# Block 2's attention heads reordered on ScalarE, weight splits behind the exponentials, and tensors moved by 64 and 160 bytes

## The chip, the core and the metric

The kernel runs on one core of a Trainium2 chip. The metric is the device time of one execution in microseconds, lower is better. The engines are TensorE (PE: matrix products, with PEld for its weight loads), VectorE (DVE), ScalarE (ACT), GpSimd (POOL) and the DMA queue that SyncE (SP) feeds.

## What is computed

The reference is a small transformer stack on 256 tokens of width 1024, in float32: two layers of a first block, then two of a second.

```python
def first_block(...):        # 2 layers
    x = x + 0.5 * swiglu(rms_norm(x), w1, w2)          # 1024 -> 2 x 2816 -> 1024
    x = x + hybrid_mixer(rms_norm(x), ...)             # LRU, latent attention, convolution
    x = x + 0.5 * swiglu(rms_norm(x), w1, w2)
def second_block(...):       # 2 layers
    mix = hybrid_mixer_2(rms_norm(x), ...)             # three kinds of attention
    x = x + rms_norm_2(mix)
    x = x + rms_norm_2(conv_ffn(rms_norm(x)))          # 1024 -> 2 x 2816, 3 taps, 2816 -> 1024
def hybrid_mixer_2(h, ...):
    o_fox = fox_attention(...)      # 4 heads, decaying bias from cumulated log_f
    o_nsa = nsa_attention(...)      # 8 heads: compressed keys (gelu MLP), selected blocks, window
    o_dil = dilated_attention(...)  # 4 heads
    return concatenate([o_fox, o_nsa, o_dil]) @ w_out
```

## The kernel before

**Products.** Activations lie as features x tokens: `h_hi` and `h_lo` hold eight tiles of 128 x 256. Every large product is made of three matmuls in a fast float32 format: weights and activations are split into a rounded part and a remainder (`w_hi`, `w_lo`, `h_hi`, `h_lo`), and `product` (L654 to 659) adds hi x hi, hi x lo and lo x hi into one PSUM bank. Each matmul loads a 128 x 128 block of weights and streams 256 columns of the activation. Some products take the weights unsplit in plain float32 (`whole_product`, L704). In `tokens_product` (L706 to 712) the roles change: an activation (`h_hi`, `win_hi`) is the loaded operand, and `w_hi` or `w_lo` is streamed.

**Weights.** All weights come as a stream of units of at most 16 blocks (1 MB). SyncE loads unit s into one of two slots of `raw` (`load_unit`, L580) once the unit two before is split. ScalarE copies it to `w_hi` (`split_hi`, L588 to 606), which waits for the load and for PE to have used the unit four before. VectorE subtracts to `w_lo` (`split_lo`, L629 to 637). PE waits for `w_lo`. The engines' programs say by hand where each split stands in its queue: `split.until(s)` splits all units up to s at that place.

**Where tensors lie.** The tensors are allocated in the order of their declarations, each start on a multiple of 32 bytes. By the program's address map `raw`, `w_hi`, `w_lo`, `x`, `h_hi`, `h_lo`, `const`, `vec`, `scr` and `sq` start at multiples of 128 bytes in each partition. `rinv` has 258 floats, so what follows it starts 32 bytes past such a multiple: `trig1`, `hid_hi`, `hid_lo` (the hidden activations of the FFNs), and, in the same space in other stages, `m_hi`, `m_lo` (block 1's merged branches), `win_hi`, `win_lo`, `o2_hi`, `o2_lo` (block 2). Tiles within them are 1024 bytes apart, blocks of weights 512.

**FFNs.** There are four of block 1 and two of block 2. Each has 22 "up" units of 16 blocks (48 matmuls over `h_hi`, `h_lo`) and 16 "down" units of 11 blocks (33 matmuls over `hid_hi`, `hid_lo`).

**Block 2's mixer.** `second_steps` (L254) writes the order of TensorE's groups by hand: for n from 0 the scores ("S", n), the transposes ("T", n-3), the product with the values ("V" or "W", n-4), and then what `MIX2_BESIDE[n]` puts beside: projections ("f", i), rotations ("R", i), the compression MLP ("ca", "cmp", "ct", "c2"), its attention ("SC", "TC", "J"), the cumulated decays ("cum"), parts of the output projection ("K", i). There are 24 heads. VectorE follows this order (`STEPS2`), ScalarE follows `EVAC2`, which is the same with two steps swapped. For a head ScalarE computes the exponential of n and scales the probabilities of n-1 (step "S", L1741 to 1744), copies the transposed probabilities ("T", L1748) and, at the end of a tile, the output ("W", L1750). "W" n must be copied before the next tile's first "V" may write its bank. VectorE makes the row maximum that the exponential waits for.

```python
EVAC2 = list(STEPS2)
for n in range(3, len(HEADS2)):
    at = EVAC2.index(("S", n))
    EVAC2[at], EVAC2[at + 1] = EVAC2[at + 1], EVAC2[at]
```

So ScalarE's order is T(n-3), S(n), V or W(n-4). In the mixer both splitters run three units ahead of the group in hand (`split.until(at2 + UNIT_OF2[g] + AHEAD)` ahead of the group's own work), and ScalarE also splits ahead of each exponential what `freed_by_scores` (L1678) allows. The units of this stage are, in order, f1, f2, f3, vb0, vb1, f0, f8, va0, va1, f4, f5, ca0, cmp0, ca1, cmp1, f6, f7, O0 to O3; "K" and "O" use O0 to O3. ScalarE's gelu in "cmp" and its exponential need different function tables, which it loads at each change.

## Time and profile before

| | |
|---|---|
| median of 3 runs | 2071.71 us (2068.88 to 2075.6) |
| the profiled execution | 2077.53 us, of which the span is 2075.7 us |
| PE, PEld busy | 1994.5 us (96%), 1898.6 us (91%) |
| DVE, ACT, POOL busy | 1395.0 us (67%), 1159.7 us (56%), 142.6 us (7%) |
| DMA | 329.80 MB, mean 159 GB/s |
| granted TensorE clock | 0.981 of full on average |

The busy time of PE is the sum of matmuls whose ends are modelled and overlap: a matmul of 0.28 us is followed by the next one 0.12 us later. So what a matmul costs is read from start to start, and from how many fall into a stretch, not from its duration. The block 1 layers take the span from 11 to 1280 us, block 2's two layers the rest; the heads of block 2's mixer lie at 1315 to 1468 and at 1710 to 1863 us.

### The profile page before, as it was taken

The page shows a single profiled execution, that of the slowest core. Times are in us where ns is not written, and L with a number is a line of the kernel's source. Part 1 is how long each engine was busy: PE and PEld are TensorE (multiplying, and loading weights), DVE is VectorE, ACT ScalarE, POOL GpSimd, SP SyncE. Part 2 cuts the span into 40 slices and gives each one's busy share as a digit, 9 for nine tenths or more (in the row PEclk, how much of TensorE's full clock was granted, in tenths as well). Part 3 has the DMA queues.
Part 4 walks back from the last instruction along what each step waited for, and adds up shares of the span by engine and source line. Part 5 has one row for each costly group of instructions (what it writes and reads, how often), then busy time and mean ns, then how long its engine had stood idle before and what let it go on. Part 6 is the DMA issues. An engine that isn't in the chain of part 4 may idle for free.

```text
span 2075.7 us, 39521 instructions
## 1 busy us (share of the span) xinstructions
PE 1994.5 (96%) x15240; PEld 1898.6 (91%) x15240; DVE 1395.0 (67%) x2058; ACT 1159.7 (56%) x1847; POOL 142.6 (7%) x153
## 2 busy tenths in 40 slices
PE   7999989999999999999999999998999999899998
PEld 7999988999999999988999999876899998679997
DVE  5765787666655665788666656775698477638963
ACT  5444676564445444676465435665666458556753
POOL 1063100010000001100010001000200010002000
PEclk9999999999999999999999999999999999899999
DMA  5545433455545545443455544531255544203643
GB/s 210 202 166 191 168 127 132 156 189 199 171 168 199 191 154 192 170 150 109 151 193 192 184 156 168 181 123 41 102 187 181 189 144 169 102 24 140 214 156 115
DMA packets 53533, 329.80 MB, mean 159 GB/s; under 512 B 5936, under 2 KB 6704, under 8 KB 27952
## 3 DMA queue, kind: packets, MB, share of 16 engines
q1 hardware_dynamic: 53424, 328.34, 45.4%
q8 instruction: 69, 1.13, 0.2%
q14 instruction: 40, 0.33, 0.0%
HBM read 327.27 MB, written 1.05 MB: 158 GB/s over the span
## 4 chain that ended last, share of the span: by engine, by line
PE 66%; DVE 10%; issue 8%; ACT 5%; DVEq 4%; DMA 4%; POOLq 3%; POOL 1%; ACTq 0%; SPq 0%
PE bank L657 17%; PE bank L658 17%; PE bank L659 17%; PE bank L704 4%; DVE w_lo L636 3%; DMA raw<-in_w 3%; ACT w_hi L597 2%; PE bank L669 1%; PE bank L671 1%; DVE conv L1371 1%; PE bank L1659 1%; PE bank L1643 1%; PE bank L678 1%; DVEq L1365 1%; PE bank L1660 1%
## 5 line engine op out<-in xcount | busy, mean ns | idle before, releaser
L636 DVE TENSOR_TENSOR w_lo<-raw,w_hi 128x2048 fp32r<-128x2048 f32 (+3 forms) x348 | 673.6, 1939 | 326.5 <-ACT w_hi L597 310.6
L657 PE MATMUL bank<-h_hi,w_hi 128*128 128x256 f32 x2704 | 779.8, 288 | 12.2 <-DVE w_lo L636 4.2
L658 PE MATMUL bank<-h_lo,w_hi 128*128 128x256 f32 x2704 | 768.2, 284 | 0.0
L659 PE MATMUL bank<-h_hi,w_lo 128*128 128x256 f32 x2704 | 768.0, 284 | 0.0
L597 ACT ACTIVATE w_hi<-raw 128x2048 fp32r<-128x2048 f32 (+2 forms) x346 | 560.5, 1623 | 138.8 <-DMA raw<-in_w 117.4
L657 PEld LDWEIGHTS bank<-h_hi,w_hi 128*128 128x128 f32 x2704 | 522.2, 193 | 17.6 <-issue 11.7
L658 PEld LDWEIGHTS bank<-h_lo,w_hi 128*128 128x128 f32 x2704 | 522.1, 193 | 1.3
L659 PEld LDWEIGHTS bank<-h_hi,w_lo 128*128 128x128 f32 x2704 | 522.0, 193 | 0.0
L657 PE MATMUL bank<-hid_hi,w_hi 128*128 128x256 f32 x1056 | 295.4, 280 | 0.0
L658 PE MATMUL bank<-hid_lo,w_hi 128*128 128x256 f32 x1056 | 295.4, 280 | 0.0
L659 PE MATMUL bank<-hid_hi,w_lo 128*128 128x256 f32 x1056 | 295.4, 280 | 0.0
L657 PEld LDWEIGHTS bank<-hid_hi,w_hi 128*128 128x128 f32 x1056 | 198.5, 188 | 0.0
L658 PEld LDWEIGHTS bank<-hid_lo,w_hi 128*128 128x128 f32 x1056 | 198.5, 188 | 0.0
L659 PEld LDWEIGHTS bank<-hid_hi,w_lo 128*128 128x128 f32 x1056 | 198.5, 188 | 0.0
L897 ACT ACTIVATE scaled<-scaled 128x256 f32<-128x256 f32 x88 | 36.8, 418 | 257.9 <-DVE scaled L944 257.9
L796 POOL TENSOR_TENSOR acc<-sq 128x256 f32<-128x256 f32 x13 | 12.2, 942 | 1549.4 <-ACT sq L789 1549.1
L1371 DVE SCALAR_TENSOR_TENSOR conv<-glu,vec,conv 128x256 f32<-128x256 f32 x240 | 106.0, 481 | 11.9 <-issue 2.8
L789 ACT ACTIVATE sq<-x 128x256 f32<-128x256 f32 (+1 forms) x88 | 35.9, 410 | 115.2 <-DVE x L974 90.8
L944 DVE TENSOR_TENSOR scaled<-bank,rinv 128x512 f32<-128x512 f32 x88 | 60.6, 689 | 44.8 <-PE bank L659 36.8
L669 PE MATMUL bank<-h_hi,w_hi 128*128 128x256 f32 x224 | 63.4, 316 | 16.0 <-DVEq L1921 6.6
L800 POOL TENSOR_TENSOR acc<-acc,sq 128x256 f32<-128x256 f32 x65 | 60.2, 926 | 222.3 <-ACT sq L789 219.1
L669 PEld LDWEIGHTS bank<-h_hi,w_hi 128*128 128x128 f32 x224 | 49.6, 222 | 18.2 <-issue 10.0
(337 smaller groups left out, 2937.3 us busy)
## 6 DMA issues: line engine op xcount, KB each, us to landing
raw<-in_w SPq DMA_DIRECT2D x198, 1024.0 KB, 4.8
raw<-in_w SPq DMA_DIRECT2D x96, 704.0 KB, 4.1
raw<-in_w SPq DMA_DIRECT2D x52, 768.0 KB, 4.2
raw<-in_w SPq DMA_DIRECT2D x8, 512.0 KB, 3.8
raw<-in_w SPq DMA_DIRECT2D x4, 576.0 KB, 3.7
x<-in_x SPq DMA_DIRECT2D x1, 1024.0 KB, 5.0
out<-x SPq DMA_DIRECT2D x4, 256.0 KB, 2.4
const<-in_const SPq DMA_DIRECT2D x1, 548.0 KB, 5.4
```

The source lines that it names most:

```text
L597: last = act.activation(w_hi[:, s % SPLIT_SLOTS, 0:parted], raw[:, s % RAW_SLOTS, 0:parted], ACT.Copy)
L636: dve.tensor_tensor(w_lo[:, s % SPLIT_SLOTS, 0:n], raw[:, s % RAW_SLOTS, 0:n], w_hi[:, s % SPLIT_SLOTS, 0:n].bitcast(F32), ALU.subtract).t ...
L657: pe.matmul(out, hi, x_hi, start=start, stop=False, skip_group_check=skip)
L658: pe.matmul(out, hi, x_lo, start=False, stop=False, skip_group_check=skip)
L659: return pe.matmul(out, lo, x_hi, start=False, stop=stop, skip_group_check=skip)
L669: pe.matmul(out, w_hi[:, s % SPLIT_SLOTS, at], h_hi[:, k], start=k == 0 and half == 0, stop=False, skip_group_check=half == 1)
L704: return pe.matmul(out, whole_part(s, block, 1), y, start=start, stop=stop)
L789: act.activation(sq[:, parity], src, ACT.Square).then_inc(nm.sq_ready.sem, 1)
L800: pool.tensor_tensor(acc[:], acc[:], sq[:, t % 2], ALU.add).then_inc(nm.sq_summed.sem, 2 if t == KT - 2 else 1)
L897: act.activation(scaled[:, parity, 0:T], scaled[:, parity, 0:T], ACT.Silu).then_inc(silu_ready.sem, 1)
L944: dve.tensor_tensor(halves(scaled[:, parity]), halves(bank[:, :]), by_r(2), ALU.mult).then_inc(work.freed["v"].sem, 1)
L1371: last = dve.scalar_tensor_tensor(conv[:, t], glu[:, t, j:j + T], w, conv[:, t], ALU.mult, ALU.add)
```

## The change

Six things change.

1. `EVAC2`: for n from 4 on, the step S(n) moves two places back instead of one, so ScalarE's order is T(n-3), V or W(n-4), S(n). Head 3 keeps its place.
2. `MIX2_BESIDE`: ("cum", 1) goes from step 13 to 15, ("R", 7) from 14 to 17 (ahead of ("K", 0)).
3. The units cmp0, ca1, cmp1, f6 and f7 no longer make ScalarE and VectorE split three ahead (`SPLIT_BESIDE`). Instead the exponentials of heads 8, 9, 10, 12, 14 are each followed on ScalarE by splits (`HIGH_BEHIND`), and the steps S 9, 10, 11, 12, 16 on VectorE (`LOW_BEHIND`). VectorE's splits up to O3 behind S 14 go.
4. ScalarE splits ahead of the exponential for heads below 8 only.
5. Two unused tensors are added: `offset_h` (64 bytes) ahead of `x`, and `offset_hid` (96 bytes) ahead of the tensors that stages share. `x`, `h_hi`, `h_lo` and all behind move by 64 bytes, `hid_hi`, `hid_lo`, `m_hi`, `win_hi`, `o2_hi` and the like by 160: by the address map all of these then start 64 bytes past a multiple of 128. `raw`, `w_hi` and `w_lo` stay.
6. For the room, `w_lat` holds 21 blocks instead of 22 (`LAT_BLOCKS` 9 instead of 10); one more block of unit ("uq", 2) goes to `sq`.

```diff
-               5: [("win", 4), ("f", 5)], 7: [("ca", 0), ("cmp", 0)], 8: [("ca", 1), ("cmp", 1)], 9: [("ct", 0)],
-               10: [("f", 6), ("c2", 0)], 11: [("cum", 0)], 12: [("SC", 0), ("f", 7)], 13: [("cum", 1), ("R", 6)],
-               14: [("R", 7), ("TC", 0)], 16: [("J", 0)], 17: [("K", 0)], 18: [("K", 1)], 20: [("J", 1)], 21: [("K", 2)], 23: [("K", 3)],
-               25: [("K", 4)], 27: [("K", 5)]}
+               5: [("win", 4), ("f", 5)], 7: [("ca", 0), ("cmp", 0)], 8: [("ca", 1), ("cmp", 1)],
+               9: [("ct", 0)], 10: [("f", 6), ("c2", 0)], 11: [("cum", 0)], 12: [("SC", 0), ("f", 7)], 13: [("R", 6)],
+               14: [("TC", 0)], 15: [("cum", 1)], 16: [("J", 0)], 17: [("R", 7), ("K", 0)], 18: [("K", 1)], 20: [("J", 1)],
+               21: [("K", 2)], 23: [("K", 3)], 25: [("K", 4)], 27: [("K", 5)]}
+HIGH_BEHIND = {8: ("f", 6), 9: ("f", 7), 10: ("O", 0), 12: ("O", 2), 14: ("O", 3)}
+LOW_BEHIND = {9: ("f", 6), 10: ("f", 7), 11: ("O", 0), 12: ("O", 2), 16: ("O", 3)}
+SPLIT_BESIDE = [("cmp", 0), ("ca", 1), ("cmp", 1), ("f", 6), ("f", 7)]
...
-    at = EVAC2.index(("S", n))
-    EVAC2[at], EVAC2[at + 1] = EVAC2[at + 1], EVAC2[at]
+    step = EVAC2.index(("S", n))
+    EVAC2.remove(("S", n))
+    EVAC2.insert(step + (1 if n == 3 else 2), ("S", n))
...
+        sbuf("offset_h", [P, 16])
         x = sbuf("x", [P, KT, T])
...
+        sbuf("offset_hid", [P, 24])
...
-                w_lat = sbuf("w_lat", [P, 22 * P], F32, early)
+                w_lat = sbuf("w_lat", [P, (12 + LAT_BLOCKS) * P], F32, early)
...
-                if g in UNIT_OF2 and kind != "O" and g != ("vb", 1):
+                if g in UNIT_OF2 and kind != "O" and g != ("vb", 1) and g not in SPLIT_BESIDE:
                     split.until(at2 + UNIT_OF2[g] + AHEAD)
...
                 elif kind == "S":
-                    split.until(freed_by_scores(at2, i))
+                    if i < 8:
+                        split.until(freed_by_scores(at2, i))
                     softmax_act_exp(act, probs2, row2, i % PROBS2, max2_ready(l, i + 1), exp2_ready)
                     for n in due(i, len(HEADS2)):
                         softmax_act_norm(act, probs2, row2, n % PROBS2, sums2_ready(l, n + 1), probs2_ready)
+                    if i in HIGH_BEHIND:
+                        split.until(at2 + UNIT_OF2[HIGH_BEHIND[i]])
...
-                    if i == 14:
-                        split.until(at2 + UNIT_OF2["O", 3])
+                    if i in LOW_BEHIND:
+                        split.until(at2 + UNIT_OF2[LOW_BEHIND[i]])
```

## Rows read from the trace of the kernel before

**Rows 1.** Windows: stretch, us, busy us (count) of PE, PEld, DVE, ACT, POOL, clock, DMA
```profile
30.00:90.00 60.00, 60.00 (x503) 60.00 (x502) 40.17 (x45) 29.46 (x34) 0.00 (x0) 1.00 0.56 196
150.00:200.00 50.00, 50.00 (x428) 50.00 (x427) 24.98 (x25) 22.30 (x26) 22.11 (x21) 1.00 0.54 185
...
1550.00:1598.00 48.00, 48.00 (x402) 48.00 (x401) 42.28 (x67) 32.90 (x46) 0.00 (x0) 1.00 0.56 189
```

**Rows 2.** Timeline of PE: start us, us, line; six starts apart, an "up" unit
```profile
59.74 0.28 PE L658 MATMUL bank<-h_lo,w_hi 128*128 128x256 f32 x1
...
60.46 0.28 PE L658 MATMUL bank<-h_lo,w_hi 128*128 128x256 f32 x1
```

**Rows 3.** The same of a "down" unit, seven starts apart
```profile
159.78 0.28 PE L658 MATMUL bank<-hid_lo,w_hi 128*128 128x256 f32 x1
...
160.60 0.28 PE L659 MATMUL bank<-hid_hi,w_lo 128*128 128x256 f32 x1
```

**Rows 4.** The same of cmp1, 41 starts apart (256 columns streamed from w_hi)
```profile
1363.60 0.28 PE L710 MATMUL bank<-w_hi,win_hi 128*128 128x256 f32 x1
...
1368.43 0.28 PE L712 MATMUL bank<-w_lo,win_hi 128*128 128x256 f32 x1
```

**Rows 5.** The same of va1, 20 starts apart (512 columns streamed from w_hi)
```profile
1327.80 0.40 PE L710 MATMUL bank<-w_hi,h_hi 128*128 128x512 f32 x1
...
1332.36 0.39 PE L712 MATMUL bank<-w_lo,h_hi 128*128 128x512 f32 x1
```

**Rows 6.** The page's costliest groups: busy us, mean ns, idle before
```profile
L657 PE MATMUL bank<-h_hi,w_hi 128*128 128x256 f32 x2704 | 779.8, 288 | 12.2 <-DVE w_lo L636 4.2
...
L657 PE MATMUL bank<-hid_hi,w_hi 128*128 128x256 f32 x1056 | 295.4, 280 | 0.0
```

**Rows 7.** Waits of PE in the whole span: us in total, times, longest
```profile
PE bank L1643 <- ACT scr L1750: 10.5, 4, 4.5
PE bank L1599 <- ACT v_own L1728: 9.1, 2, 4.6
```

**Rows 8.** Timeline of ACT at 1366 to 1375 us
```profile
1366.89 1.92 ACT L597 ACTIVATE w_hi<-raw 128x2048 fp32r<-128x2048 f32 x1 [2.17 <-DMA raw<-in_w]
...
1371.70 1.89 ACT L597 ACTIVATE w_hi<-raw 128x2048 fp32r<-128x2048 f32 x1
1373.62 1.28 ACT L1728 ACT_TABLE_LOAD   x1
1374.91 0.38 ACT L1728 ACTIVATE v_own<-bank 128x256 f32<-128x256 f32 x1
```

**Rows 9.** Timeline of DVE at 1409 to 1414 us
```profile
1409.30 2.28 DVE L636 TENSOR_TENSOR w_lo<-raw,w_hi 128x2048 fp32r<-128x2048 f32 x1
1411.67 0.69 DVE L1801 TENSOR_TENSOR sq<-bank,sin 128x512 f32<-128x512 f32 x1
```

**Rows 10.** Timeline of ACT at 1414 to 1417 us
```profile
1414.93 0.40 ACT L1034 ACTIVATE probs<-probs,row 128x128 f32<-128x128 f32 x1 [3.51 <-DVE row L1029]
...
1416.52 0.36 ACT L1750 ACTIVATE scr<-bank 128x256 f32<-128x256 f32 x1
```

**Rows 11.** Timeline of PE at 1416 to 1423 us
```profile
1416.93 1.10 PE L1643 MATMUL bank<-scr,v2b 128*64 128x256 f32 x2 [4.46 <-ACT scr L1750]
...
1418.39 2.08 PE L1649 MATMUL bank<-p_cmp_t,v_own 128*128 128x256 f32 x4
...
1422.84 0.36 PE L1659 MATMUL bank<-o_hi,w_hi 128*128 128x256 f32 x1 [0.19 <-DVE o_lo L1911]
```

**Rows 12.** Windows of the stretches at low clock in the heads, columns as Rows 1
```profile
1372.40:1382.60 10.20, 7.25 (x26) 5.22 (x27) 8.34 (x19) 10.00 (x20) 0.00 (x0) 0.51 0.55 201
1416.80:1420.20 3.40, 3.27 (x8) 1.92 (x8) 0.00 (x0) 2.02 (x8) 0.00 (x0) 0.53 0.00 0
1768.40:1775.10 6.70, 6.10 (x20) 4.06 (x21) 6.06 (x19) 6.52 (x15) 0.00 (x0) 0.51 0.49 186
1809.40:1819.50 10.10, 9.40 (x28) 6.14 (x29) 2.95 (x9) 5.38 (x17) 0.00 (x0) 0.51 0.01 2
```

More of the change, by code:

```diff
@@ L36 @@
 FFN_AHEAD = 4
+LAT_BLOCKS = 9
 EPS = 1e-6
@@ L339, in build @@
                 lat = sbuf("lat", [P, 5, T], F32, early)
-                w_lat = sbuf("w_lat", [P, 22 * P], F32, early)
+                w_lat = sbuf("w_lat", [P, (12 + LAT_BLOCKS) * P], F32, early)
             o1 = sbuf("o1", [P, 4, T], F32, phase)
-            sbuf("rest", [P, 3, 4, T], F32, phase)
+            sbuf("rest", [P, T + (12 + LAT_BLOCKS) * P], F32, phase)
             pad_r = sbuf("pad_r", [P, 4, T + LRU_TAPS - 1], F32, phase)
@@ L557, in build @@
         hid2_ready = signal("hid2_ready", FT)
-        LAT_BLOCKS = 10
         def unit_kind(s):
@@ L572, in whole_part @@
             if unit == ("uq", 2) and block >= LAT_BLOCKS:
-                return sq[:, 0, (block - LAT_BLOCKS) * P:(block - LAT_BLOCKS + blocks) * P]
+                return sq[:].rearrange("p a t -> p (a t)")[:, (block - LAT_BLOCKS) * P:(block - LAT_BLOCKS + blocks) * P]
             if unit[0] == "uq":
@@ L1684, in freed_by_scores @@
             due_ = [UNIT_OF2[g] + AHEAD for step in range(n + 1) for g in MIX2_BESIDE.get(step, []) if g in UNIT_OF2]
-            last = UNIT_OF2["O", 3] if n > 12 else max(due_)
+            last = max(due_)
             while s < at2 + last and stream.used[s + 1 - SPLIT_SLOTS][2] < mark["S", n]:
@@ L1784, in mixer2_dve @@
                 out = work.out(g)
-                if g in UNIT_OF2 and kind != "O" and g not in (("vb", 1), ("f", 0)):
+                if g in UNIT_OF2 and kind != "O" and g not in (("vb", 1), ("f", 0)) and g not in SPLIT_BESIDE:
                     split.until(at2 + UNIT_OF2[g] + AHEAD)
```

## The prediction

> **What bounds the kernel now.** I read the windows of the FFN stretches first. In each of them PE is busy all the time at full clock, VectorE 50 to 88% and ScalarE 45 to 69% [rows 1]. So two thirds of the span are set by how fast PE issues matmuls, and nothing else. Then I read what one matmul costs there, from start to start. In an "up" unit six starts lie 0.72 us apart, 120 ns each [rows 2]; over 60 us the count gives the same, (503 less 2.4 that overlap the window's edge) in 60 us, 119.9 ns [rows 1]. In a "down" unit seven starts take 0.82 us, 117.1 ns [rows 3]; over 50 us 425.6 matmuls, 117.5 ns [rows 1]. I use 117.4. Both stream 256 columns, with the same blocks of weights. What differs is where the streamed tensor starts: by the address map `h_hi` lies like `w_hi`, at a multiple of 128 bytes, `hid_hi` 32 bytes past one. cmp1, where the stationary operand is 32 bytes off and the streamed one is not, gives 4.83 us over 41, 117.8 ns [rows 4]. And 512 columns with both at multiples of 128 take 4.56 us over 20, 228 ns [rows 5]. That is 108 ns for 256 more columns, so 12 of the 120 ns belong to the matmul and not to its columns, and 9 to 10 where the operands are shifted against each other.
>
> Next the waits of PE. Two in block 2's heads come in both layers and are the largest after the opening of the kernel: 9.1 us in two before ("ct", 0) for ScalarE's gelu, and 10.5 us in four before a "V" for ScalarE's copy of "W", two of them 4.5 us [rows 7]. [...]
>
> **The change part by part.**
>
> *The shift against the weights (item 5).* After it `h_hi`, `h_lo`, the hidden, merged and output tensors and the windows all lie 64 bytes from the phase of `w_hi`. No row shows this distance. From above it is bounded by 120 ns, as at distance 0; from below by 108 ns, the columns alone [rows 5]. Between them I take 115 ns: a shift of 32 takes 2.6 off the 12, in either operand's favour [rows 3, 4], so the loss falls with the distance, and distance 64 is the farthest two starts can be apart modulo 128; twice 2.6 is 5.2. I choose this as the continuation of the two values I have, not as something shown. The sum:
> - "up" matmuls of six FFNs: 6 x 22 x 48 = 6336, at 120 - 115 = 5.0 ns: 31.7 us. PE is the bound there. In block 2 VectorE has 42.28 us of work in 48 us [rows 1], 5.05 us for a unit of 5.76, and the unit would take 5.52: it stays hidden.
> - "down" matmuls: 6 x 16 x 33 = 3168 (1056 a line, three lines [rows 6]) at 2.4 ns: 7.6 us.
> - the mixers: `h` takes part in 8112 matmuls of `product` (2704 a line, three lines [rows 6]) and by the program in 1440 more, 9552; less 6336 that is 3216, at 5.0 ns 16.1 us. Another 960 (`m_hi`, `o2_hi`, `win_hi`) at 2.6 ns: 2.5 us. PE waits for others in the mixers in places, so only 0.6 of these 18.6 us is counted, my choice: 11.2 us.
> Together 50.5 us.
>
> *ScalarE's splits at cmp (items 3, 4).* ct needs cmp1's gelu. Before it ScalarE copies a unit that it had to wait 2.17 us for (the load came at 1366.89), loads a table, does an exponential, copies another unit at 1371.70 for 1.89 us, loads the other table for 1.28 us and ends the gelu at 1375.29 [rows 8]. PE ended cmp1 at 1368.43 + 0.28 [rows 4], and its next work, head 9's scores and what goes with them, ends at about 1370.7 (the gelu's end less the wait of 4.6 us [rows 7]). After the change one of the two copies (f6) is left between the gelus, its load is long done, and the gelu can end about 1368.7 + 1.28 + 0.38 = 1370.4. The wait of 4.5 us falls to between 0 and 1.5 us; I take 0.7, gain 3.8 a layer. What comes next: f6 needs its `w_lo`, now behind head 9 on VectorE, a 2.28 us instruction [rows 9] which I put at 1372.0 to 1374.3, while PE arrives at 1373.6: 0.7 us of new wait. The splits of f7 and O0 now stand behind exponentials, so the copies of ct and of transposes behind them wait 1.9 us more; PE has f6's 5.5 us to cover that. Net 3.1 us a layer.
>
> *ScalarE's copies first, (R, 7) later (items 1, 2).* At 1411.67 VectorE starts (R, 7), right behind a `w_lo` of 2.28 us [rows 9]; head 15's maximum comes after both, so ScalarE sits 3.51 us and starts the exponential at 1414.93, and only then the copy of W 11 at 1416.52 [rows 10], for which PE waits 4.46 us with head 12's values [rows 11]. After the change that copy stands ahead of the exponential and its input is ready at about 1411.5: the wait goes, 4.5 us a layer. The other two waits on this copy are (10.5 - 9.0)/2 = 0.75 us each and go too. What is late next: `w_lo` of O3 now stands behind head 16, ahead of (J, 0)'s addition. Today (J, 0) ends at 1420.4 and (K, 0) starts at 1422.84 with 0.19 us of wait [rows 11], so the chain addition, copy, subtraction just fits. With 2.28 us in front of it, less about 1.1 us for (R, 7)'s and head 17's matmuls and what VectorE is ahead, I count 1.2 us of new wait, between 0 and 2.5. The exponential itself is now 0.36 us later each head; the transposes it feeds are a step away, so nothing. Net 4.5 + 0.8 - 1.2 = 4.1 us a layer.
>
> *The clock.* In the four stretches at low clock PE is busy 7.25 + 3.27 + 6.10 + 9.40 = 26.0 us [rows 12]; at full clock the same takes 13 us less. They start within 5 us of the waits named. Without these waits I count 60% as regained, 7.8 us; the bounds are 0 and 13.
>
> Heads together: 2 x (3.1 + 4.1) + 7.8 = 22 us, with bounds of 8 and 31.
>
> *Item 6* moves one block of a unit that is used in place; the number of ScalarE's instructions stays. ("cum", 1) at step 15 fills a step that had nothing beside it; its bias is first used by head 18, three steps on, so I cost it at nothing; without that cover it would be the 1.2 us of its four additions on VectorE, once a layer.
>
> **The sum.** 50.5 + 22.2 = 72.7 us off the profiled execution's 2077.5 us gives 2004.8. The median of the runs shown, 2071.7, is 5.8 us lower, so I forecast 2071.7 - 72.7 = 1999 us.
>
> [...]
>
> **The rivals.**
> 1. *Any shift does what 32 bytes does.* Two shifted cases, two near values (117.4 and 117.8) [rows 3, 4], speak for it; that one streams `hid`, the other `w_hi`, doesn't tell how it goes on with distance. Then `h` gains 2.6 ns: (6336 + 0.6 x 3216) x 2.6 = 21.5 us, "down" nothing. With 22: 2028 us.
> [...]
> 3. *It isn't the shift, or its period is 64 bytes.* "Up" and "down" differ in more than the address (other instructions run beside them), which speaks for it; that each stretch shows one steady spacing, in all layers, speaks against it. If nothing moves, the heads alone give 2050 us; with a period of 64 the 117.4 go to 120 also and cost (3168 + 0.6 x 960) x 2.6 = 9.7 us: 2059 us.
> 4. *Slower than before.* At distance 64 PE's two streams meet worse than at 0. A mean of 123 ns costs 6336 x 3 + 3168 x 5.6 + 0.6 x (3216 x 3 + 960 x 5.3) = 45.6 us against 22 from the heads: 2095 us. It decides from a rise of about 1.5 ns above 120. No row has such a spacing in a steady stretch; only that the distance is untried speaks for it.
>
> That the change doesn't do what it says concerns the heads: if the waits only move (f6's `w_lo`, (K, 0)), their 22 us shrink to 8. It lies inside each case.
>
> **How the numbers follow.** Chances: forecast 0.46, rival 1 0.21, rival 2 0.16, rival 3 0.12, rival 4 0.05. The likeliest case alone spans 2014 (heads 8) to 1985. The range goes from 1950, which holds most of rival 2, to 2045, beyond rival 1 with weak heads; left out are rivals 3 and 4 and the rest of 2, 2 in 10. A difference of 0.3% (6 us) is about what can be told. Slower by more than that: rival 4, and 0.01 of rival 3 with heads that lose, 0.06. Within it: rival 3 with heads near the lower bound, 0.03. Faster: 0.91.
>
> **What would show it.** [...] The waits for L1728 and L1750 below 1.5 us each; no clock below 0.9 in the heads; new waits of PE at f6's first matmul and at L1659. Wrong would make me: VectorE as the bound of block 2's "up" units, loads that come late for "down" units at the faster pace, and another large wait in the heads.

## The result and the profile after

The changed kernel takes 2056.25 us (median; 2050.62 to 2060.32), the kernel before on the same chips 2073.25 us: a ratio of 0.9915, with a 95% interval of 0.989 to 0.994. That is 17 us off, where 73 were forecast. The sign was right, the size was not, and 2056 lies outside the range. The profiled execution took 2058.2 us with a span of 2056.4 us, 19.3 us shorter than the one of before. The times of whole kernels below are medians too; one execution of the six of e9_distance_112 took 3209 us at a granted clock of 0.56 and is left out.

First the windows of the same FFN stretches as in [rows 1]; the columns are the stretch, its length, the busy time and count of PE, PEld, VectorE, ScalarE and GpSimd, the clock, and the DMA share and rate.

```profile
30.00:90.00 60.00, 60.00 (x512) 60.00 (x511) 40.91 (x45) 30.02 (x35) 0.00 (x0) 1.00 0.58 203
150.00:200.00 50.00, 50.00 (x427) 50.00 (x426) 26.16 (x25) 21.90 (x25) 21.28 (x19) 1.00 0.52 178
1537.00:1585.00 48.00, 48.00 (x410) 48.00 (x409) 42.18 (x67) 32.82 (x46) 0.00 (x0) 1.00 0.56 187
```

Less the 2.4 that overlap the edge, "up" makes 509.6 matmuls in 60 us, 117.7 ns each, and 117.8 in block 2; "down" 424.6 in 50 us, 117.8 ns. So "up" won 2.2 ns instead of 5.0, and "down" lost 0.3 instead of winning 2.4. The timeline of an "up" unit shows the same, 0.71 us for six starts, from 59.67 to 60.38 us (0.72 in [rows 2]).

Not every stretch over `h` shows this value, though. The units f6 and f7 of layer 0, with the same operands at the same distance, run at 113.3 ns (21 starts in 2.38 us), and so do a few other stretches, in the mixers and in the first products of two "up" parts, about one in twenty of all over `h`:

```profile
1360.32 0.28 PE L662 MATMUL bank<-h_hi,w_hi 128*128 128x256 f32 x1
...
1362.70 0.28 PE L662 MATMUL bank<-h_hi,w_hi 128*128 128x256 f32 x1
```

Then PE's waits in the whole span (us in total, times, the longest). Neither of the two of [rows 7] is left. What has grown or is new:

```profile
PE bank L662 <- DVE w_lo L641: 8.4, 4, 2.8
PE bank L1642 <- ACT scr L1756: 7.4, 6, 2.5
...
PE bank L1664 <- DVE sq L1809: 1.8, 2, 1.1
```

19.6 us of large waits went. In their place stand 7.4 us at the transposes (L1642), 4.2 us more at units that wait for their `w_lo` (8.4 after 4.2), 3.3 of them f6's, and 1.8 us at (K, 0). And the low clock, which was to go with the waits, has grown in layer 0, to 27 us in one piece after 13.7 in two (in layer 1 it is 10 us after 17):

```profile
1386.00:1413.00 27.00, 24.73 (x74) 15.53 (x73) 17.37 (x44) 12.73 (x38) 0.00 (x0) 0.50 0.18 66
```

What each stage of the program takes, by the starts of PE's matmuls in the two profiled executions (the first "up" part is counted from the start of the span; the sums differ by 18.8 of the spans' 19.3 us):

| stage | before, us | after, us | won | forecast |
|---|---|---|---|---|
| six "up" parts with their norms | 811.6 | 801.5 | 10.1 | 31.7 |
| six "down" parts | 370.8 | 372.6 | -1.8 | 7.6 |
| block 1's mixers, two | 496.4 | 491.1 | 5.3 | about half of 11.2 |
| block 2's mixers, layer 0 / 1 | 191.5 / 193.6 | 192.7 / 187.2 | -1.2 / 6.4 | 22 and half of 11.2 |

So of some 54 us that are missing, 31 are in the FFNs, where only the spacing was to gain, and 22 in block 2's mixers, most of them in the heads. The experiments take the two apart.

### The profile page after: what moved, and what is told of

Same layout as the page of the kernel before. It is cut to its first block, busy times and chain, and to the rows that moved or that the text cites. A ratio compares the mean times of both kernels' runs of the same rounds, so it can differ in the third digit from the quotient of the medians.

```text
span 2056.4 us, 39523 instructions
## 1 busy us (share of the span) xinstructions
PE 1975.5 (96%) x15240; PEld 1874.6 (91%) x15240; DVE 1392.9 (68%) x2058; ACT 1159.1 (56%) x1847; POOL 141.3 (7%) x153
## 4 chain that ended last, share of the span: by engine, by line
PE 74%; DVE 11%; ACT 5%; DVEq 4%; DMA 3%; issue 3%; POOL 1%; POOLq 0%; SPq 0%; ACTq 0%
PE bank L662 19%; PE bank L664 19%; PE bank L663 19%; DVE w_lo L641 4%; PE bank L709 4%; DMA raw<-in_w 3%; ACT w_hi L602 1%; DVE conv L1376 1%; PE bank L1648 1%; PE bank L674 1%; PE bank L676 1%; PE bank L1664 1%; PE bank L683 1%; DVE x L1938 1%; PE bank L1642 1%
## 5 line engine op out<-in xcount | busy, mean ns | idle before, releaser
L662 PE MATMUL bank<-h_hi,w_hi 128*128 128x256 f32 x2704 | 770.9, 285 | 18.0 <-DVE w_lo L641 8.4
L663 PE MATMUL bank<-h_lo,w_hi 128*128 128x256 f32 x2704 | 758.7, 281 | 0.0
L664 PE MATMUL bank<-h_hi,w_lo 128*128 128x256 f32 x2704 | 758.4, 280 | 0.0
L662 PEld LDWEIGHTS bank<-h_hi,w_hi 128*128 128x128 f32 x2704 | 510.9, 189 | 23.2 <-issue 14.6
L663 PEld LDWEIGHTS bank<-h_lo,w_hi 128*128 128x128 f32 x2704 | 510.5, 189 | 1.2
L664 PEld LDWEIGHTS bank<-h_hi,w_lo 128*128 128x128 f32 x2704 | 510.9, 189 | 0.0
L674 PE MATMUL bank<-h_hi,w_hi 128*128 128x256 f32 x224 | 59.3, 303 | 17.5 <-DVEq L1929 6.6
L674 PEld LDWEIGHTS bank<-h_hi,w_hi 128*128 128x128 f32 x224 | 46.3, 207 | 20.6 <-issue 10.0
```

The lines of the kernel that those rows point to most:

```text
L662: pe.matmul(out, hi, x_hi, start=start, stop=False, skip_group_check=skip)
L663: pe.matmul(out, hi, x_lo, start=False, stop=False, skip_group_check=skip)
L664: return pe.matmul(out, lo, x_hi, start=False, stop=stop, skip_group_check=skip)
L674: pe.matmul(out, w_hi[:, s % SPLIT_SLOTS, at], h_hi[:, k], start=k == 0 and half == 0, stop=False, skip_group_check=half == 1)
```

## Experiments on the spacing

**One half of the change each.** e1_offsets_only is the kernel before with the two empty tensors and what makes room for them; e2_heads_only is the kernel after without the tensors.

```diff
+        sbuf("offset_h", [P, 16])
         x = sbuf("x", [P, KT, T])
...
+        sbuf("offset_hid", [P, 24])
```

> The kernel before with the moved tensors alone (items 5 and 6 of the change). In the trace of the changed kernel the spacing of matmuls over h is 117.6 ns instead of 120.0, over hid 117.8 instead of 117.3. Theory A (the shift is what gained): 6336 x 2.4 = 15.2 us in the up units, less 3168 x 0.4 = 1.3 us, plus some 4 us in the mixers: 0.991 to 0.992 of the kernel before, as much as the whole change. Theory B (the order of the heads gained, the faster matmuls wait elsewhere): 0.998 or more.

> The changed kernel without its two offset tensors, so all starts as before (items 1 to 4 and 6). Theory A: the heads give nothing that can be told, 0.998 to 1.001. Theory B: 0.991 to 0.993. My prediction had 22 us for this part, 0.989. Its waits of PE for the gelu and for the copy of W should be as small as in the changed kernel; the spacing over h 120.0 ns.

Measured: the placement alone 2064.59 us, ratio 0.9952 (0.9935 to 0.9969); the heads alone 2068.94 us, 0.9981 (0.997 to 0.9991). The product is 0.9933, which lies within the interval of the whole, so the two add up to it as far as can be told. Placement gave 8.5 us where 50.5 were forecast, the heads 4 where 22 were.

**The disputed cost by itself.** A kernel of its own runs groups of 48 matmuls in the form of the kernel's products (weights' high part against both parts of the activation, low part against the high one), nothing beside them; the transformer is left out. Only where the activation starts changes from group to group.

```diff
+CASES = [("sweep", "product", H + d, 2 * H + d, 0) for d in range(0, 1056, 32)]
...
+                                last = pe.matmul(into, w[wi][:, block_at:block_at + P], a[ai][:, k * N:k * N + N], start=start, stop=stop,
```

> A kernel of its own that measures the spacing alone: it loads one input, fills weights and activations with its rounded values, and issues 55 groups of 48 matmuls on an otherwise idle core; the reference's computation is left out. Groups differ in where the streamed activation starts against the loaded weights: 0 to 1024 bytes in steps of 32, and some with hi and lo apart, with both moved by 64, with fixed activation, and with the roles swapped. Theory 1 (any shift that isn't 0 does the same): 120.0 ns at 0, 117.3 to 117.8 at all others. Theory 2 (it depends on the distance modulo 256 or more): 120.0 at 0, 117.6 at 64, and about 113.6 at 192, which is where the output projection of the changed kernel lies and what it shows. Theory 3 (the address itself matters, not the distance): the group with both moved by 64 shows 117.6 instead of 120.0.

Measured, as means of the last 35 steps of a group at full clock, by the distance of the streamed start from the stationary one in bytes: 0: 120.0 ns (its last 20 steps; the very first group ran at low clock in part), 32: 117.8, 64: 117.8, 96: 120.1, 128: 118.7, 160: 118.7, 192: 117.8, 224: 118.3, and the same eight values again and again up to 1024. With weights and activation moved together by 64 bytes, distance 0 stays at 120.0 and 64 at 117.8. So it is the distance and not the address, and it counts modulo 256, not 128. Rival 3 falls, and so does the thought on which 115 rested, that a distance of 64 is the farthest two starts can be apart: nothing falls with the distance. Two kinds of group fell out of line. With the roles swapped the groups at 64 and 192 gave 113.3 ns once they were steady; in these groups the loaded block moves by 128 bytes from product to product, so that both take 64 and 192 in turn, and they are not one distance. With 512 columns, where the activation is the loaded operand and starts so many bytes behind the streamed weights, 0 gave 226.7 ns and 64 gave 233.4, which is what the 512-column products of the kernel after show (233.3 after 227.6).

**Other orders of blocks, and what went before.** In the kernel after, the output products (K, O) run at 113.3 to 113.6 ns at distance 192, all but one group of them (117.8), where this first sweep had 117.8.

> A kernel of its own, which leaves the reference's computation out: 55 groups of 48 matmuls of 256 columns, as in the first such run, with other orders of blocks. Open from there: the K and O products stream o2 at 113.6 ns in the kernel after (distance 192) and 117.4 before (32), which one tile streamed at 192 with weights in a row didn't show (117.8). Theory A (the distance decides, the order of blocks only with it): the out order gives 113.5 at 64 and 192, 117.4 at 32, 120 at 0; weights in a row or one bank take it back to 117.8. Theory B (what matters is how a stretch begins): the out order shows 117.8 at 64 and 192 too, and the groups that begin behind 1 to 5 small matmuls differ among each other, by up to 1.5 ns, at the same distance. For the other orders: with w_lo moved by 64 the third matmul of a triple has its own distance, and I expect a mean between 117.8 and 120; hi-hi, lo-hi, hi-lo like the present order, 120 and 117.8; 16 and 48 bytes between their neighbours, 118 to 119.

Measured: theory A of that text falls, since banks, halves, slots, far or equal blocks and the order of the three products change nothing (120.0, 117.8 and 117.8 at 0, 64 and 192, but for the first group, which ran at low clock in part). Theory B holds in part: at 0 and 64 it doesn't matter in these groups what went before, at 160 five small matmuls ahead of the group turn 118.7 into 117.3. The weights' low part moved by 128 bytes turned 117.8 at 64 into 113.3. New are the distances between: 16 and 112 gave 113.3 ns, 80 gave 119.9.

**The fine sweep.**

```diff
+CASES = [("product", H + d, 2 * H + d, 0, 0) for d in range(0, 256, 4)]
```

> A kernel of its own, which leaves the reference's computation out: groups of 48 matmuls of 256 columns, with the distance between the streamed and the stationary operand in steps of 4 bytes over 256, then distances 16 and 112 behind 1, 3 and 5 small matmuls, and 16, 48, 112, 144, 240 with the roles swapped and with 512 columns. If the spacing is a number of starts that meet in the memory, it takes few values (113.3, 117.8, 120.0 and mixtures) and 16 and 112 belong to bands some 8 to 16 bytes wide; if 113.3 was an accident of how those two groups began, the groups behind small matmuls show 117 to 120 for the same distance. For 512 columns 227 at 16, against 226.7 at 0 and 233.4 at 64. A spacing under 113 would be new.

Measured: at 112 bytes 113.3 ns in each of the four groups here and in the one before, whatever ran ahead. At 144 and 192 one group shows 113.3 and another 118.7 or 117.8; at 16 there were 113.3, 116.6 and 118.7, at 32 116.6 and 117.8, over the two sweeps of this kind and the first. Distances that are no multiple of 8 lie at 116.9 to 123.8. Nothing lies below 113.3. The timeline shows it, by two starts of the same product 36 matmuls apart, at 64 and at 112 bytes (4.24 and 4.08 us: 117.8 and 113.3 ns):

```profile
134.94 0.28 PE L93 MATMUL bank<-act,w_lo 128*128 128x256 f32 x1
139.18 0.28 PE L93 MATMUL bank<-act,w_lo 128*128 128x256 f32 x1
...
203.98 0.28 PE L93 MATMUL bank<-act,w_lo 128*128 128x256 f32 x1
208.06 0.28 PE L93 MATMUL bank<-act,w_lo 128*128 128x256 f32 x1
```

So a distance has one to three steady spacings. Where there are several, what ran ahead changed the value in some groups (16 and 160 bytes); that the start of the stretch picks it is the likely reading, not a shown one. And an untried distance need not lie between its neighbours: 80 and 96 bytes show 120, 112 shows 113.3, 128 shows 118.7.

**Carried into the kernel.** e7_sixteen asks for 16 bytes with a smaller tensor:

```diff
-        sbuf("offset_h", [P, 16])
+        sbuf("offset_h", [P, 4])
```

> [...] In the matmuls alone a distance of 16 gave 113.3 ns a matmul, 64 gave 117.8 and 0 gave 120.0. Theory A (the distance modulo 256 sets the spacing in the kernel as in the matmuls alone): h and hid at 113.3 ns; 6336 x 4.3 + 3168 x 4.4 = 41 us in the FFNs, and 2 to 8 us in the mixers, against after's 2056: 2007 to 2015 us. Theory B (in the kernel PE's spacing is set by what else reads the memory; the steady 117.6 to 117.8 of the kernel after is a floor that other engines set): no change, 2050 to 2060. Theory C (the spacing falls, but the time goes to VectorE and the loads, 5.05 us of work in a unit of 5.44): half of it, about 2030.

Measured: 2050.25 us, 0.9877 (0.986 to 0.9894). The expectation had a flaw, it counted with 16 bytes: by this kernel's address map `x` starts 32 bytes behind the start of the 16-byte tensor, so h and the hidden tensors lay at 32, the output tensors and the windows at 160. Those at 32 show 116.7 ns in the kernel, in the same steps of 113, 116, 117 and 120 as the group at 32 in the fine sweep; the output products show 117.2 to 118.9, where the sweeps had 117.3 and 118.7 at 160. So the kernel follows the sweep, and theory B of that text falls.

e9_distance_112 is the kernel after with only its operands placed again: h, the hidden, the merged and the output tensors start at 112 bytes, as views into a slightly longer tensor, the windows at 192.

```diff
+        def pair(name, tiles, skip, stack=ctx):
+            both = sbuf(name, [P, skip + 2 * tiles * T], F32R, stack)
...
-        h_hi = sbuf("h_hi", [P, KT, T], F32R)
-        h_lo = sbuf("h_lo", [P, KT, T], F32R)
+        h_hi, h_lo = pair("h_pair", KT, 28)
```

> [...] In the matmuls alone 112 gave 113.3 ns in all of its five groups, whatever went before, while 64 gave 117.8, 0 gave 120.0, and 16, 32, 144, 160 and 192 gave two or three different values, by what went before. Theory A (the kernel's spacing is this spacing, and my 115 ns was a value between two that exist): h and hid at 113.3 ns, 6336 x 4.3 + 3168 x 4.4 = 41 us in the FFNs, 4 to 10 us in the mixers, tokens with 512 columns unchanged at 233: 2056 less 45 to 51, 2005 to 2011 us. Theory B (in block 2, and where ScalarE and VectorE are 70 to 90% busy, something else is due at 5.44 us a unit): the spacing falls to 113.3 in block 1, units of block 2 wait; 2015 to 2035 us. Theory C (what went before matters in the kernel even at 112): no steady 113.3, 2040 to 2055 us.

Measured: 2022.76 us, 0.9742 (0.973 to 0.9755), 53 us less than before. Its windows of the "up" stretches, block 1 and block 2:

```profile
30.00:90.00 60.00, 60.00 (x531) 60.00 (x531) 40.44 (x45) 30.11 (x35) 0.00 (x0) 1.00 0.56 201
...
1516.00:1564.00 48.00, 48.00 (x426) 48.00 (x425) 44.73 (x69) 34.19 (x49) 0.00 (x0) 1.00 0.57 197
```

That is 528.6 in 60 us, 113.5 ns, and 423.6 in 48 us, 113.3 ns: theory A for the spacing, in block 2 too, with VectorE at 93%. The total is 33 us below after's by the medians (36 by the ratios), not 45 to 51, as theory B had it in sum, but its reason covers only a part. The waits for `w_lo` grew from 8.4 to 15.5 us, and 5.5 of them are a single new one in the first "down" part (at 173.71 us), which took 67.9 us where the other five took 59.7: 5.5 us of wait, and the low clock behind it. That is most of what "down" lacks: it won 6 us on after where 14 were forecast. Neither the loads nor the subtractions hold it up. ScalarE does, which stands 14.25 us at a square of the norm, with the weight copies queued behind, for a sum on GpSimd; and GpSimd is still at the sine table until 168.8 us:

```profile
169.07 0.72 POOL L802 TENSOR_TENSOR acc<-sq 128x256 f32<-128x256 f32 x1 [0.23 <-issue]
169.92 0.42 ACT L795 ACTIVATE sq<-x 128x256 f32 x1 [14.25 <-POOL acc L802]
```

In the kernel after ScalarE stands there for 7.61 us and PE doesn't notice. No run has moved this table.

## Experiments on the heads

**The two parts of the heads apart.** e5_order_only has ScalarE's copies first and the steps spread anew (items 1 and 2), e4_splits_only has the weight splits behind the heads (items 3 and 4). Both start from the kernel before.

```diff
-    EVAC2[at], EVAC2[at + 1] = EVAC2[at + 1], EVAC2[at]
...
+    EVAC2.remove(("S", n))
+    EVAC2.insert(step + (1 if n == 3 else 2), ("S", n))
```

> The kernel before with items 1 and 2 alone (ScalarE copies transposes and values ahead of the next head's exponential; (R, 7) at step 17, (cum, 1) at 15), the weight splits as before. The prediction gave this part 4.1 us a layer and a share of the clock: 2073 - 8 - 4 = 2061 us. My theory now is the same for this part: the 4.6 us in front of (V, 12) go in both layers, the wait of 4.6 us in front of ct stays, (K, 0) waits 1.3 us: 2062 to 2066 us. Rival: these heads lose at half clock what the wait gives, as in the run with the heads' part whole (24 and 17 us of half clock against 14 and 17): 2069 to 2073 us.

> The kernel before with items 3 and 4 alone (the weight splits of f6, f7 and O stand behind exponentials and maxima of heads 8 to 16), ScalarE's order of copies and the steps beside the heads as before. The prediction gave this part 3.1 us a layer and a share of the clock. My theory now: the 4.6 us in front of ct go in both layers, f6 waits 1.8 us a layer in their place, and the subtractions ahead of SC bring 2 to 4 us of new waits a layer: near zero net, 2067 to 2074 us against 2073. Rival, the prediction's: -6.2 us and a part of the clock's 7.8, 2063 us.

Measured: order 2063.38 us, 0.9942 (0.9926 to 0.9959); splits 2071.8 us, 0.9987 (0.9972 to 1.0002). Both together (e2_heads_only) are 0.9981: slower than the order alone, by 0.4%. So the order alone was worth 12 us, as the prediction had it (8.2 and a share of the clock's 7.8). The splits, forecast at 6.2 us and their share, gave 3 us alone, with an interval of the ratio that takes in 1, and on top of the order they took two thirds of its gain away again. The waits of PE in layer 0's heads, order alone first, then splits alone:

```profile
PE bank L1600 <- ACT v_own L1729: 4.6, 1, 4.6
PE bank L1650 <- ACT scr L1749: 1.3, 1, 1.3
PE bank L1660 <- DVE sq L1802: 1.1, 1, 1.1
```

```profile
PE bank L1640 <- ACT scr L1754: 5.3, 3, 3.7
PE bank L1646 <- ACT scr L1756: 1.7, 2, 0.9
PE bank L660 <- DVE w_lo L639: 1.7, 1, 1.7
```

The order took the wait in front of (V, 12) away and left the one in front of ct (L1600). The splits took that one away, and f6's 1.7 us and some 1.6 us at the transposes (L1640) came in its place; the largest wait at the transposes, 3.7 us at 1414.74 us, with 0.9 us behind it at (V, 12), is the old one in front of (V, 12), met one step earlier. Over the heads of each layer (from 70 us behind the mixer's start to its end, in the profiled executions):

| kernel | waits of PE, us, layer 0 / 1 | low clock, us | whole mixer, us |
|---|---|---|---|
| before | 10.0 / 9.9 | 13.7 / 17.1 | 191.5 / 193.6 |
| e1, placement alone | 10.4 / 9.7 | 23.9 / 17.1 | 195.3 / 191.2 |
| e5, order alone | 7.3 / 7.2 | 10.2 / 10.2 | 187.1 / 187.4 |
| e4, splits alone | 9.6 / 10.1 | 13.7 / 13.7 | 190.8 / 191.1 |
| e2, both | 6.7 / 6.6 | 23.9 / 17.1 | 192.9 / 190.6 |
| after | 6.7 / 7.1 | 27.3 / 10.2 | 192.7 / 187.2 |
| e3, subtractions later | 8.0 / 6.6 | 10.2 / 23.9 | 185.5 / 190.6 |
| e6, subtractions early | 4.2 / 3.2 | 13.7 / 10.2 | 184.3 / 183.0 |
| e12, with 112 bytes | 3.5 / 3.6 | 10.2 / 6.8 | 184.2 / 181.6 |

Two things can be read here. Order and splits together have no more wait than the order alone, 6.7 after 7.3; each removed large wait was for the most part replaced by small ones. And what makes both together slower is the clock: 41 us at half after 20, in which PE was busy, so that about half of the 21 us is lost, the 9 us by which the two mixers differ (383.5 after 374.5). These are single executions, but the others agree: the granted clock of the whole span is 0.988 in the mean of the order's four and 0.984 in that of the eleven with both, and 0.0036 of 2070 us are 7.5 us, of the 8 by which the ratios differ. With the order alone PE meets its one large wait ahead of f6, and f6's 48 matmuls follow; with both, the waits lie between the small matmuls of heads 12 to 14, and the low clock lasts until (K, 0). Whether it is the kind of work behind the waits that decides is not shown; no run here has changed that alone.

Where the new waits come from is in the timelines of the kernel after, VectorE and ScalarE, then PE:

```profile
1378.31 2.29 DVE L641 TENSOR_TENSOR w_lo<-raw,w_hi 128x2048 fp32r<-128x2048 f32 x1 [3.25 <-ACT w_hi L602]
1381.20 2.29 DVE L641 TENSOR_TENSOR w_lo<-raw,w_hi 128x2048 fp32r<-128x2048 f32 x1 [0.59 <-ACT w_hi L602]
1384.94 0.42 ACT L1742 ACTIVATE p_cmp<-p_cmp 128x256 f32<-128x256 f32 x1 [3.77 <-DVE p_cmp L1857]
1385.26 0.47 ACT L1756 ACTIVATE scr<-bank 128x384 f32<-128x384 f32 x1
1385.78 0.75 PE L1642 MATMUL bank<-const,probs 128*128 128x128 f32 x3 [2.51 <-ACT scr L1756]
```

O1's and O2's subtractions stand ahead of the compressed softmax (SC) on VectorE, so that SC starts at 1383.40 us. It is not only their 4.6 us: ahead of them VectorE stands idle for 3.25 and 0.59 us (the brackets), since it waits for ScalarE's copies of the same two units while SC is queued behind. ScalarE comes to SC's exponential, has to wait 3.77 us for it, and the transposes' copy is queued behind; PE waits for that copy. The prediction looked at who waits for ScalarE's copies and not at what the subtractions were put in front of.

**Moving the subtractions.** e3_low_later is the kernel after with them behind SC:

```diff
-LOW_BEHIND = {9: ("f", 6), 10: ("f", 7), 11: ("O", 0), 12: ("O", 2), 16: ("O", 3)}
+LOW_BEHIND = {9: ("f", 6), 10: ("f", 7), 11: ("O", 0), 13: ("O", 1), 14: ("O", 2), 16: ("O", 3)}
```

> The kernel after, with one edit: VectorE's weight subtractions of O1 and O2 no longer both stand behind head 12's maximum, ahead of the compressed softmax (SC), but behind those of heads 13 and 14. In the kernel after PE waits 2.5, 0.3 and 1.2 us at the transposes and scores behind SC in layer 0 (0.8, 0.8, 0.6 and 1.7 us in the run with the heads' part alone), and the low clock (half) that begins there lasts 27 us in layer 0 and 10 us in layer 1. Theory A (these two subtractions delay SC, ScalarE waits for SC in front of the transposes' copy, PE waits for the copy, and the clock falls in consequence): those waits fall below 0.5 us each, the low stretch shortens by at least half, and the time falls by 6 to 20 us against after, to about 2043 us; VectorE's work is then nearest to a bound, (K, 0) waits 1 to 3 us. Theory B (VectorE is simply short of time in heads 12 to 17, wherever the splits stand): the wait moves to heads 14 and 15 and (K, 0), same low clock, time within 4 us of after's 2056. Theory C (the low clock comes from these heads' own thin work, not from the waits): waits go, 3 to 5 us, but the low stretch of 20 us or more stays; 2052 us.

Measured: 2052.67 us, 0.9893 (0.9876 to 0.9909). Against after, in the profiled executions, layer 0 won 7 us and layer 1 lost 3: in both a new wait of 3.2 us, for a transposes' copy that stood behind O3's weight copy on ScalarE, and in layer 1 24 us of low clock. None of the three theories came out as written.

e6_low_early puts them early instead, f6 behind head 8, f7 and O0 behind 10, and only O1 between head 12 and SC:

```diff
+HIGH_BEHIND = {8: ("f", 6), 9: ("f", 7), 10: ("O", 0), 11: ("O", 1), 12: ("O", 2), 14: ("O", 3)}
+LOW_BEHIND = {8: ("f", 6), 10: ("O", 0), 12: ("O", 1), 14: ("O", 2), 16: ("O", 3)}
```

> The kernel after, with the weight splits of the heads set again: ScalarE's copy of O1 stands behind head 11's exponential instead of head 12's; VectorE's subtractions of f6 behind head 8, f7 and O0 behind head 10, O1 behind 12, O2 behind 14. Putting both O1 and O2 later only moved the wait: O3's load starts when O1's subtraction has read its buffer, ScalarE then waits for that load with the transposes' copy behind it, and PE waited 3.7 us there. Theory A (each subtraction also starts a load, and ScalarE's copy that waits for the load holds up the transposes; so the subtractions must come early, except the one ahead of the compressed softmax): f6's wait of 1.8 us and the 3 to 4.5 us around the compressed softmax go, (K, 0) keeps 1 to 2 us, the half clock in the heads falls from 27 and 10 us to under 10 a layer: 2056 less 12 to 22, 2034 to 2044 us. Theory B (VectorE is the bound of heads 12 to 17, whatever the order): 2048 to 2054 us, with new waits at (K, 0).

Measured: 2047.71 us, 0.9853 (0.9839 to 0.9868), 8.5 us below after by the medians and 13 by the ratios. f6's wait and those around SC went; 2.2 us stay at the transposes, and 14 and 10 us of low clock. Theory A's waits came out, its time only in part. One reason in that text was wrong: e3's late copy of O3 had not waited for its load (1392.83 us has no such wait) but for VectorE's maximum of head 14, 3.78 us.

**The last copy.** With the placement at 112, O3's copy on ScalarE was put behind head 15 (e8_both), ahead of head 14's exponential, where ScalarE sat idle for 1.6 us (e10_in_the_gap), and behind head 14 as in e6 (e12_first_setting).

> The same placement at 112 together with the splits set again: ScalarE's copies of O1 behind head 11 and of O3 behind head 15, VectorE's subtractions of f6 behind head 8, f7 and O0 behind 10, O1 behind 12, O2 behind 14. With the first such setting (O3 behind 14) the waits up to 1389 us went, and one of 2.2 us stayed where the transposes' copy of head 12 stood behind O3's copy on ScalarE. Theory A (that copy is the last thing in the way): its wait goes, the half clock in the heads falls to under 7 us a layer, and the heads give 8 to 16 us against the placement alone. Theory B (VectorE bounds heads 12 to 17): waits of 2 us or more at the next transposes or at (K, 0), and the heads give what they gave before, 6 to 9 us. With theory A of the placement: 1990 to 2002 us, the fastest kernel of this study.

> The kernel e8_both with one edit: ScalarE's copy of O3 no longer stands behind head 15's exponential but ahead of head 14's. In e8_both head 13's transposes were copied only at 1368.7 us, behind that copy of 1.89 us (1366.87), and PE waited 3.0 us for their bank at the chain products (J, 0), in both layers; the half clock behind it lasted 17 and 14 us. Ahead of head 14's exponential ScalarE sits idle for 1.6 us anyway, waiting for VectorE's maximum. Theory A (the transposes' copy is the thing that PE can't do without, and a weight copy costs nothing only where ScalarE would wait for VectorE): the 3 us go in both layers, half clock in the heads under 7 us a layer, 8 to 14 us less than e8_both, 2005 to 2011 us, and all of the heads' first forecast is there. Theory B (each such gap is taken from VectorE's slack, so the wait moves on): another wait of 2 us or more at heads 14 to 17, 2015 to 2019 us.

> The placement at 112 with the splits as in the run that first set them early (ScalarE's copy of O3 behind head 14 instead of 15); nothing else differs from e8_both. That setting gave 13 us against after, at distance 64; e8_both gave 5 us against the placement alone. Theory B (VectorE, without a pause of more than 1.3 us between the maximum of head 12 and (K, 0), is the bound of heads 12 to 17, and the place of O3's copy only chooses who waits): within 4 us of e8_both and e10, 2014 to 2022 us, with 2 to 3.5 us of waits in heads 14 to 16 in each layer. Rival (the place behind 14 is the right one, and 15 and the gap are worse by 4 us a layer): 2008 to 2013 us, and waits below 1.5 us.

Measured: 2018.69 us, 0.9719 (0.9705 to 0.9732); 2018.33 us, 0.9728 (0.9714 to 0.9743); 2014.81 us, 0.9698 (0.9677 to 0.9719). Each has a wait of 2.0 to 3.0 us per layer somewhere in heads 13 to 16; it only changes its place. In e10 it is at (J, 0), and VectorE shows why: from head 12's maximum on, until 1379 us, its work has no pause of over 1 us. The windows of that kernel are heads 13 to 17 and what follows:

```profile
1355.00:1379.00 24.00, 21.30 (x106) 14.24 (x105) 21.23 (x49) 15.85 (x43) 0.00 (x0) 0.85 0.34 115
1379.00:1400.00 21.00, 19.84 (x105) 14.77 (x105) 7.66 (x19) 9.56 (x31) 0.00 (x0) 0.85 0.05 19
```

VectorE is busy 21.2 of 24 us in the first and 7.7 of 21 right behind. So the work in this stretch is near VectorE's limit, and in the three settings tried a split that was moved within it was paid for by another step. That VectorE is the bound there is argued from this; no run has taken work off it in this stretch alone. e12 is the fastest kernel of the study, 61 us (3.0%) below before; whether its 4 us against the other two are real can't be told from intervals that overlap.

## Why the prediction failed, step by step

- **What bounds the kernel.** Right for the FFN's steady stretches, though the six FFNs are 1182 of the 2075.7 us, 57% and not two thirds. Wrong as a rule for the whole "up" part: in block 2 the steps between matmuls that are longer than 160 ns held, beyond one spacing each, 12.0 and 11.7 us of a part's 140 in before and 14.2 and 13.8 in after, so each of its two parts gave back all but 0.1 or 0.2 of the 2.3 us that the spacing won. Over all six parts these gaps grew from 34.1 to 39.0 us; 6336 x 2.2 ns = 13.9 us less 4.9 are, but for 1 us, the 10 of the table. The prediction counted each nanosecond of spacing in full.
- **The shift, 115 ns.** This is the step that failed: the term of 50.5 us, its 5.0 ns a matmul over `h` and 2.4 over `hid`, where 2.2 and a loss of 0.3 were measured. The premise (a shift of 32 takes 2.6 off, in either operand's favour) was a correct reading of two rows. The continuation was not: at 64 the measured value is 117.8 but for a few stretches, as at 32, and the period is 256, so that [rows 3] (distance 160) and [rows 4] (32 with the roles swapped) were two points of another curve. Rival 1 named the spacing that was measured at 64, and 2028 us; but its rule, that any shift does what 32 bytes does, falls too (80 and 96 bytes show 120, 112 shows 113.3), so that it met this value is luck. Against its 21.5 us the placement alone won 8.5, which is less by the gaps above, by "down" (-1.8), and by the mixers, where the spacing won 5 us in block 1 and in block 2 nothing that the low clock left. Rival 2 (chance 0.16, and with it the range's lower end of 1950) stood for a distance of 64 without any of the loss; no run shows its spacing: 117.8 was measured there, and the fastest of any group is 113.3 ns. Rival 4 had no case: 123 ns exists, but at distances such as 4 and 180.
- **ScalarE's splits at cmp, 3.1 us a layer.** The wait in front of ct went (4.6 to nothing, forecast 0.7), and f6's new wait was 1.65 us where 0.7 was forecast. Not seen was the queue on VectorE ahead of SC: 2.5, 0.3 and 1.2 us in layer 0. Of waits in the heads the change took 3.3 and 2.8 us a layer in all where 7.2 were forecast for this step and the next.
- **ScalarE's copies first, 4.1 us a layer.** Right as a sum, in part by luck: e5 gives 12 us for both layers and their clock, but the waits fell by 2.7 us a layer and not by 4.1, since 1.6 us at the chain products (L1650) came in, and the clock gave the rest. The forecast 1.2 us of new wait at (K, 0) came out at 1.1, but for another reason. PE waits not for O3's `w_lo` and the chain's addition but for a bank: (R, 7), now right ahead of (K, 0), has to be read by VectorE first, and its releaser is that reading (`sq`, L1809 in after), not `o_lo`.
- **The clock, 7.8 us.** It did not come back with the waits. In the profiled executions the time at half clock in the heads went from 31 to 38 us (31 to 20 with the order alone). This term differs between executions of one kernel: the granted clock of the whole span lay between 0.979 and 0.986 in 18 executions of before, which is 29 us of half clock more or less. In the means it is 0.983 for before, 0.984 for e2 and 0.982 for after, so next to nothing was regained with the heads as a whole; with the order alone it is 0.988.
- **The range.** 1950 to 2045 took the lower bound of the heads (8 us) and rival 1 (21.5 us) as its worst case; the heads gave 4 and the placement 8.5. The likeliest case's lower end doesn't follow from its terms: 2071.7 less 50.5 and 31 is 1990, not 1985. VectorE's work in a unit of block 2, by its own row, is 42.28 / 48 x 5.76 = 5.07 us, not 5.05. Neither changes the forecast.

## What to carry to other kernels

Where two operands start relative to each other is worth measuring with a small kernel of its own before it is set: here a sweep in steps of 4 bytes, half a millisecond of chip time, found 6.7 ns a matmul where the change got 2.2, and a value between two measured ones would have been a guess at any distance. A step that is moved out of one engine's way is put in front of something on another: read, for both engines, what is queued behind its new place, what it has to wait for there, and whether that stretch has idle time at all. When PE gets faster, look again at engines that were never in the way: GpSimd's sine table in the first "down" part cost nothing at 117.8 ns a matmul and 8 us at 113.3. And a gain in a steady stretch counts only up to the next producer; take the gaps of the whole part, not of its best window.

## What the runs showed of the hardware that was not expected

- The spacing of 256-column matmuls depends on the distance between streamed and stationary start modulo 256 bytes: 113.3 ns at 112, 117.8 at 64 for the most part, 120.0 at 0, 118.9 to 121.3 at the multiples of 8 that are not of 16, up to 123.8 at 132. In the sweeps it didn't change when both operands moved by 64 bytes, nor with the bank, the half, or the order of blocks (tried at 0, 64 and 192).
- At some distances there are two or three steady spacings, each of which lasts for the whole stretch: 16, 32, 144, 160 and 192 in the sweeps, and 64 in the kernel (117.8, and 113.3 in f6, f7 and other units of the mixers). 192 gave 117.8 in a group of one run and 113.3 in one of another, and 113.3 to 113.6 in most of the kernel's output products. At 112 the small kernel and the FFNs showed 113.3 alone, the output products of e9 114.1 to 115.1 from a group's fourth matmul on. What sets these values was not found.
- 512 columns want another distance: with the loaded operand 0 or 240 bytes behind the streamed one 226.7 ns, at 192 228.8, at 128 232.4, at 16, 48, 64, 112 and 144 233.3 to 233.4.
- In the heads the clock stayed at its lower level (granted clock 0.50) for 3.4 to 27 us in one piece after waits that together were shorter than 6 us; the longest piece, 27.3 us, lies in heads 12 to 16 of the kernel after.
